# An attention mixer on one NeuronCore: recurrent projections from the first attention's end, the second attention's values last, no idle wide products, and 64-row products for two heads in turn

## Chip and metric

One core of a Trainium2 chip runs the whole program. The metric is the device time of one execution in microseconds (us), as the median over runs. TensorE multiplies (granted clock 1.2 or 2.4 GHz), VectorE and ScalarE do elementwise work, GpSimd some of it, and SyncE issues the loads of weights.

## What is computed

512 tokens of width 1024 in float32 pass two hybrid layers, a feed-forward layer, one mixer layer and another feed-forward layer. The change lies in the mixer layer. Its projections `p = u @ w_in` feed a pooling, two gated linear attentions (called `hgrn` and `gla`) and an RWKV-7 recurrence, each of four heads of 64:

```python
p_pool, p_hg, p_rw, p_gla = jnp.split(p, [G, 5 * G, 5 * G + RWKV_COLS], axis=-1)
# gated linear attention, for each chunk of 64
b = jnp.cumsum(gc, axis=-2)
scores = einsum(qc, kc, exp(b_t - b_s) for s <= t)
o = scores @ vc + (qc * exp(b)) @ S
# RWKV-7, for each token
S = S * w_t - (S kk_t)(kk_t * a_t)^T + v_t k_t^T ;  o_t = S r_t
```

For the recurrence the projections are mixed with those of the token before (`rwkv_mu`); the decay goes through tanh, a 64-wide product, a sigmoid and an exponential, `a` through a product and a sigmoid, the gate through a sigmoid and a 128-wide product, and the keys are normalised for each head.

## The kernel before

Everything is written by hand: each engine has its own instruction list, in its own order, and waits for the others at named events. Each engine runs its list in order. What one list has in front of an instruction therefore delays it, whether it depends on it or not.

A wide projection is one "unit" of weights (128 x 1024 float32). SyncE loads it to one of four `raw` buffers, ScalarE rounds it (`w_high`), VectorE takes the rest (`w_low`), both up to three units ahead (`use()`), and TensorE does 24 products with 512 moving columns, three for each of eight k tiles. `projected()` makes 128 features for all tokens; `token_major()` makes the values, four units into four PSUM banks that it holds until the last unit is done.

The eight banks go round in order (`take(key, freed_by)`): TensorE waits until the named event has freed the next one.

`linear_attention(name, fill)` works through nine levels, `ORDER` = 32, 16, 8, 4, 2, 1, 64, 128, 256 (the distance of the blocks that a level connects). For a level n VectorE makes the differences of the summed decay (`logs`), ScalarE their exponential (`factor`), VectorE the product with keys and queries (`factors`), TensorE the scores of pairs of blocks (`scores`), and VectorE (sizes up to 64, a predicated copy into `sb_near`) or ScalarE (128 and 256, into `sb_far`) takes them out. The near products, blocks on the diagonal, come first; the mixed products with the values `v2` come last. Between levels `fill(n)`, n = 0 to 9, puts other work in: one wide unit on TensorE as a rule, and what that unit asks of the other engines. Level n+1's factors are made, then `fill(n+1)` runs, then `scores(n)`. The factors have two buffers, `sb_E`.

Before, `fill_hgrn` has the first attention's values (4 units), the pooling's output products, the second attention's five feature projections, and at n = 8 and 9 two units of the second attention's values. `fill_gla` has the other two value units and the eight recurrent projections within n = 0 to 5. For n = 6 to 9 it runs `operand_steps()`: decay, gates, norms and exponentials of the recurrence, with no wide unit. In that part and behind it TensorE also does products that nobody reads (`keep_busy`, 128 x 512 float32): three ahead of the last level, one after it, five after the mixed products.

Then `inverse()`: for each head the gram products `AT` and `X` (64 contraction rows, 4 tiles of 128 x 128 columns), transposes of the operands (`turn_operands`), and VectorE's masks of them onto presets that ScalarE writes. Then five sizes 2 to 32, each with `Pm`, `X` and `XT` products for each head. `side_products()` puts the grams `A_ak`, `M_rk`, `M_rb` and the product `Gv` between them. Then `recurrence()`, eight chunks, with the output projection between.

A head of 64 rows sits on rows 0 to 63 or 64 to 127 of the array (`head_tile`): even and odd heads are on different halves. In the `scores` of sizes up to 64 two heads already go in turn, product by product. In the near, far and gram products one head's products all come before the next head's. A float32 product leaves two records in the trace.

Of the kernel before, what the change touches and what calls it, by code (L numbers as in the profile page):

```python
# [35 lines left out]
ORDER = (32, 16, 8, 4, 2, 1, 64, 128, 256)  # L36
HALF_E = math.exp(-0.5)
ROUND = 12582912.0
HEADS = range(4)
LAYERS = 2  # L40
# [101 lines left out]
def unit_order(t):  # L142
# [23 lines left out]
    values, projections = mixer_group(1), mixer_tiles(*range(2, 10))  # L166
    order += values[0:3] + [projections[0], values[3]] + projections[1:]
# [19 lines left out]
class Memory:  # L187
# [71 lines left out]
    def mixers(self, region, rotary_at, xg_at, phase_at, end):  # L259
# [8 lines left out]
        m.ga = r.room("ga", SEQ)  # L268
        m.y_tok = {name: r.room(f"y_{name}", TT, G) for name in ("hgrn", "rwkv", "gla")}
        first_at = r.at  # L270
        m.operands = {}
        for name in ("hgrn", "gla"):
# [3 lines left out]
            if name == "hgrn":  # L276
                second_at = r.at
        factors_at = r.at
# [11 lines left out]

        r = region(first_at, second_at)
        m.mixed = r.room("mixed", 8, SEQ)
        m.shifted = r.room("shifted", 2, SEQ)
        r = region(xg_at, phase_at)
        m.kkE, m.rE, m.bI, m.kI = (r.room(n, 2, SEQ) for n in ("kkE", "rE", "bI", "kI"))
        tok_at = r.at
        m.tokA, m.tokB = r.room("tokA", TT, 512), r.room("tokB", TT, 512)
        r = region(tok_at, phase_at)
        m.sigma, m.cum, m.a_gate, m.tmp = (r.room(n, 2, SEQ) for n in ("sigma", "cum", "a_gate", "tmp"))
# [4 lines left out]
        r = region(first_at, kept_at)  # L304
        m.M_rk, m.M_rb = (r.room(n, 4, TT * P) for n in ("M_rk", "M_rb"))
# [105 lines left out]
def tensor_engine(e, s, mem, units):  # L411
# [334 lines left out]
    def keep_busy(n):  # L746

        i = take(("unread", turn[0]), None)
        for _ in range(n):
            e.matmul(banks[i][:, :], mem.ones, mem.inv_rms, start=True, stop=True)  # L750

    def mixers():
# [1955 lines left out]
```

## Time and profile before

| | us |
|---|---|
| median of 3 runs | 1781.59 (1779.49 to 1781.84) |
| profiled execution, its own time | 1780.97 |
| its span | 1779.2 |
| TensorE busy in the span | 1716.0 (96%) |
| VectorE, ScalarE busy | 875.6, 675.5 |

The span runs from the first to the last instruction of the profiled execution; all times below are counted from its start. The changed part lies between about 1003 and 1313 us. TensorE's "busy" includes the products nobody reads.

### The profile page before, as it was taken

The numbers are of one execution on the slowest core, as the hardware profiler recorded it, in microseconds if no ns is written. First come the engines' busy times: TensorE is split into PE (matmuls) and PEld (weight loads), VectorE is DVE, ScalarE is ACT, GpSimd is POOL, SyncE is SP. The second block draws the span as 40 slices with busy tenths as digits, with TensorE's granted clock in tenths as the row PEclk, the third lists the DMA queues.
The fourth block names the chain that finished last, engine by engine and source line by source line (L and its number), as shares of the span: only waits on it lengthen the run. The fifth ranks groups of instructions, "written<-read, shape, count | busy, mean of one in ns | idle before, by whom it ended". The sixth has DMA issues, their size and how long they took to land.

```text
span 1779.2 us, 22284 instructions
## 1 busy us (share of the span) xinstructions
PE 1716.0 (96%) x8770; PEld 1396.2 (78%) x8770; DVE 875.6 (49%) x1169; ACT 675.5 (38%) x1017; POOL 129.3 (7%) x126
## 2 busy tenths in 40 slices
PE   7999999999999899999999899989998899999997
PEld 6777778878778788888888688868987688888886
DVE  5633445633445565444334676765345554444333
ACT  5145564225555333333223553463132433333221
POOL 0001002001000100000002200001320200000000
PEclk9999999999999999999999899987999999999998
DMA  5422213322212233233333222100011223223331
GB/s 187 129 71 72 83 48 97 120 92 84 71 61 73 70 107 95 95 100 96 96 96 134 71 63 68 60 19 1 1 30 36 83 90 100 95 98 96 91 98 57
DMA packets 40745, 143.92 MB, mean 81 GB/s; under 512 B 4816, under 2 KB 4832, under 8 KB 40384
## 3 DMA queue, kind: packets, MB, share of 16 engines
q1 hardware_dynamic: 37008, 130.87, 22.9%
q0 software_dynamic: 2192, 8.73, 1.6%
q10 hardware_dynamic: 1440, 2.88, 0.4%
q8 instruction: 70, 1.15, 0.3%
q14 instruction: 35, 0.29, 0.1%
HBM read 140.37 MB, written 2.10 MB: 80 GB/s over the span
## 4 chain that ended last, share of the span: by engine, by line
PE 84%; DVE 10%; ACT 4%; issue 1%; DMA 0%; POOL 0%; DVEq 0%; ACTq 0%; SPq 0%
PE bank L450 23%; PE bank L451 22%; PE bank L452 22%; PE bank L432 8%; PE bank L438 2%; DVE sb_w_low L1133 2%; PE bank L789 1%; DVE sb_rot L1133 1%; PE bank L668 1%; PE bank L647 1%; PE bank L604 1%; DVE sb_xg_low L1141 1%; ACT sb_w_high L1872 1%; DVE sb_x L1133 1%; PE bank L527 0%
## 5 line engine op out<-in xcount | busy, mean ns | idle before, releaser
L1133 DVE TENSOR_TENSOR sb_w_low<-sb_raw,sb_w_high 128x1024 fp32r<-128x1024 f32 (+1 forms) x253 | 310.0, 1225 | 390.0 <-ACT sb_w_high L1872 384.0
L450 PE MATMUL bank<-sb_xg_high,sb_w_high 128*128 128x512 f32 x1176 | 468.1, 398 | 23.5 <-DVE sb_xg_low L1141 15.6
L451 PE MATMUL bank<-sb_xg_low,sb_w_high 128*128 128x512 f32 x1176 | 460.8, 392 | 0.0
L452 PE MATMUL bank<-sb_xg_high,sb_w_low 128*128 128x512 f32 x1176 | 460.8, 392 | 0.0
L1872 ACT ACTIVATE sb_w_high<-sb_raw 128x1024 fp32r<-128x1024 f32 (+1 forms) x253 | 263.4, 1041 | 354.7 <-PE bank L452 324.2
L450 PEld LDWEIGHTS bank<-sb_xg_high,sb_w_high 128*128 128x128 f32 x1176 | 222.4, 189 | 89.2 <-issue 31.0
L452 PEld LDWEIGHTS bank<-sb_xg_high,sb_w_low 128*128 128x128 f32 x1176 | 222.4, 189 | 47.7
L451 PEld LDWEIGHTS bank<-sb_xg_low,sb_w_high 128*128 128x128 f32 x1176 | 222.6, 189 | 44.3
L452 PE MATMUL bank<-sb_h_high,sb_w_low 128*128 128x512 f32 x352 | 136.9, 389 | 0.0
L450 PE MATMUL bank<-sb_h_high,sb_w_high 128*128 128x512 f32 x352 | 136.9, 389 | 0.0
L451 PE MATMUL bank<-sb_h_low,sb_w_high 128*128 128x512 f32 x352 | 136.9, 389 | 0.0
L2440 POOL TENSOR_TENSOR sb_square_sum<-sb_square_sum,sb_square 128x512 f32<-128x512 f32 x34 | 45.3, 1333 | 958.3 <-ACT sb_square L1872 882.2
L450 PE MATMUL bank<-sb_w_high,sb_xg_high 128*128 128x512 f32 x256 | 103.9, 406 | 0.5 <-DVE sb_w_low L1133 0.4
L451 PE MATMUL bank<-sb_w_low,sb_xg_high 128*128 128x512 f32 x256 | 100.6, 393 | 0.0
L452 PE MATMUL bank<-sb_w_high,sb_xg_low 128*128 128x512 f32 x256 | 100.3, 392 | 0.0
L451 PEld LDWEIGHTS bank<-sb_h_low,sb_w_high 128*128 128x128 f32 x352 | 66.1, 188 | 13.8
L452 PEld LDWEIGHTS bank<-sb_h_high,sb_w_low 128*128 128x128 f32 x352 | 66.1, 188 | 13.8
L450 PEld LDWEIGHTS bank<-sb_h_high,sb_w_high 128*128 128x128 f32 x352 | 66.1, 188 | 13.5
L1872 ACT ACTIVATE sb_h_high<-sb_up 128x512 fp32r<-128x512 f32 x44 | 27.8, 633 | 118.4 <-DVE sb_up L1133 118.4
L1133 DVE TENSOR_TENSOR sb_up<-bank,sb_inv_rms 128x512 f32<-128x512 f32 x44 | 30.4, 692 | 81.2 <-PE bank L452 80.6
L1872 ACT ACTIVATE sb_gate<-sb_gate 128x512 f32<-128x512 f32 x44 | 27.8, 633 | 95.2 <-DVE sb_gate L1133 95.2
L450 PEld LDWEIGHTS bank<-sb_w_high,sb_xg_high 128*128 128x128 f32 x256 | 48.5, 189 | 19.2 <-issue 8.2
(336 smaller groups left out, 2110.1 us busy)
## 6 DMA issues: line engine op xcount, KB each, us to landing
sb_raw<-w_ffn_in SPq DMA_DIRECT2D x88, 512.0 KB, 3.3
sb_raw<-w_ffn_out SPq DMA_DIRECT2D x32, 512.0 KB, 3.5
sb_raw<-w_tok SPq DMA_DIRECT2D x24, 512.0 KB, 3.9
sb_raw<-w_mix_f SPq DMA_DIRECT2D x18, 512.0 KB, 3.3
sb_raw<-w_rot SPq DMA_DIRECT2D x16, 512.0 KB, 3.7
sb_raw<-w_qk SPq DMA_DIRECT2D x16, 512.0 KB, 3.3
sb_raw<-w_out SPq DMA_DIRECT2D x16, 512.0 KB, 3.3
sb_raw<-w_ffn_out SPq DMA_DIRECT2D x16, 384.0 KB, 3.1
```

What stands on the lines that cost most here:

```text
L432: made = e.matmul(out, lhsT, rhs, start=n == 0, stop=n == len(pairs) - 1)
L438: made = e.transpose(banks[i][:, blk(n)], in_, mem.ident)
L450: e.matmul(out, w[0], v[0], start=first, stop=False)
L451: e.matmul(out, w[0], v[1], start=False, stop=False)
L452: return e.matmul(out, w[1], v[0], start=False, stop=last)
L604: made = e.matmul(out[k], m.feat["rk"][r, f, blk(j)], m.feat["rq"][r, f, j * P:], start=part == 0, stop=part == 1)
L647: e.matmul(out[k], m.qT[r, j, blk(q)], m.kT[r, j, 0:keys], start=True, stop=True).then_inc(*p.up("scores", n, 2 * j + k, q))
L668: made = e.matmul(out[64 * k:64 * k + 64, blk(q)], m.tok["av"][:, key, h * ATT_DIM:(h + 1) * ATT_DIM], m.probT[:, 2 * (q % 2) + k, blk(key ...
L789: made = e.matmul(banks[i][:, at:at + 64].rearrange("p (n c) -> p n c", c=size), et, halves(et, size, True), start=True, stop=True)
L1133: e.tensor_tensor(out, a, b, op).then_inc(*v.up(*signal))
L1872: e.activation(out, in_, func, bias=bias, scale=scale, accum_out=accum).then_inc(*a.up(*signal))
L2440: e.tensor_tensor(out, a, b, op).then_inc(*g.up(*signal))
```

## The change

- The recurrent projections come in the order 6, 7, 2, 3, 0, 1, 4, 5 (features: decay and `a`, gate, keys, receptance, values). Two take the places n = 8 and 9 of `fill_hgrn`, six n = 0 to 5 of `fill_gla`. The second attention's four value units take n = 6 to 9 of `fill_gla`.
- `operand_steps` is taken apart. Its steps stand at single n: decay and gate products at the end of the first attention, sigmoids with n = 0 of the second, decay sums n = 1, key squares and exponentials n = 2, key norm n = 3, key spread n = 5, keys n = 6 and 7, receptance n = 8 and 9. Some operands get other places in memory. The second attention's output copy on ScalarE waits for `rE`.
- `keep_busy` is gone.
- Near, far and gram products go through two heads in turn, tile by tile.
- In the first attention ScalarE does `fill(0)` ahead of `factor(0)`.
- The second attention's output gate (Silu) moves from `fill_gla(4)` to behind its root in the inverse.

The diff, cut:

```diff
+RWKV_ORDER = (6, 7, 2, 3, 0, 1, 4, 5)
-    values, projections = mixer_group(1), mixer_tiles(*range(2, 10))
-    order += values[0:3] + [projections[0], values[3]] + projections[1:]
+    order += mixer_tiles(*(2 + f for f in RWKV_ORDER)) + mixer_group(1)
@@ TensorE, attention
             fill(0)
-            for h in HEADS:
-                r, g = head_tile(h)
-                i = take(("near", name, h), ("near", name, h))
-                p.wait_ge(*of("decay summed", name, 1))
+            p.wait_ge(*of("decay summed", name, 1))
+            for two in HEAD_PAIRS:
+                out = [take(("near", name, h), ("near", name, h)) for h in two]
                 for t in range(TT):
-                    group(banks[i][:, blk(t)], [(k2[r, g, blk(t)], q2[r, g, blk(t)])], "near product", name, h)
+                    for h, i in zip(two, out):
+                        r, g = head_tile(h)
+                        made = e.matmul(banks[i][:, blk(t)], k2[r, g, blk(t)], q2[r, g, blk(t)], start=True, stop=True)
+                        if t == TT - 1:
+                            made.then_inc(*p.up("near product", name, h))
...
-                    for h in HEADS:
-                        r, g = head_tile(h)
-                        i = take(("pairs", name, n, h), ("far", name, n, h))
-                        if size == 128:
-                            for k, key in enumerate((0, 2)):
-                                group(banks[i][:, blk(k)], [(x2[r, g, blk(key)], x2[r, g, blk(key + 1)])],
-                                      "pairs", name, n, h)
-                        else:
-                            for key in range(2):
-                                group(banks[i][:, key * 256:(key + 1) * 256],
-                                      [(x2[r, g, blk(key)], x2[r, g, 256:512])], "pairs", name, n, h)
+                    for two in HEAD_PAIRS:
+                        out = [take(("pairs", name, n, h), ("far", name, n, h)) for h in two]
+                        for k in range(2):
+                            for h, i in zip(two, out):
+                                r, g = head_tile(h)
+                                if size == 128:
+                                    made = e.matmul(banks[i][:, blk(k)], x2[r, g, blk(2 * k)], x2[r, g, blk(2 * k + 1)],
+                                                    start=True, stop=True)
+                                else:
+                                    made = e.matmul(banks[i][:, k * 256:(k + 1) * 256], x2[r, g, blk(k)],
+                                                    x2[r, g, 256:512], start=True, stop=True)
+                                if k:
+                                    made.then_inc(*p.up("pairs", name, n, h))
-                if name == "gla" and n == len(ORDER) - 1:
-                    keep_busy(3)
                 scores(n)
-            if name == "gla":
-                keep_busy(1)
             fill(len(ORDER))
             last = len(ORDER) - 1
             for half in range(2):
                 i = take(("mixed", name, half), ("mixed landed", name, half))
                 p.wait_ge(*of("near done", name))
-                p.wait_ge(*of("far", name, last, 3))
-                p.wait_ge(*of(landed("v", 3), name, 3))
+                p.wait_ge(*of("far", name, last - 1 + half, 3))
@@ TensorE, fills
+                next(values_h if n < 3 else others if n < 8 else projections)
+            if n == 9:
+                decay_and_gate_in()
 
         linear_attention("hgrn", fill_hgrn)
...
+            next(projections if n < 6 else values_g)
+            if n == 1:
+                gate_out()
+            if n == 3:
+                key_norm()
+            if n == 6:
+                key_turned()
+            if n == 9:
+                p.mark("xg read", MIX_NORM)
         linear_attention("gla", fill_gla)
-        keep_busy(5)
@@ TensorE, inverse
+        def gram(what, two, left, right):
+
+            out = [take((what, h), {"AT": ("XT made", 2, h), "X": ("X made", 2, h)}.get(what, (what, h))) for h in two]
             p.wait_ge(*of(*before_products))
             for t in range(TT):
-                group(banks[i][:, blk(t)], [(left[r, f, blk(t)], right[r, f, blk(t)])], what + " product", h)
+                for h, i in zip(two, out):
+                    r, f = head_tile(h)
+                    made = e.matmul(banks[i][:, blk(t)], left[r, f, blk(t)], right[r, f, blk(t)], start=True, stop=True)
+                    if t == TT - 1:
+                        made.then_inc(*p.up(what + " product", h))
...
+        for two in HEAD_PAIRS:
+            gram("AT", two, m.bI, m.kkE)
+            if not two[0]:
+                bonus_sums(0)
+                bonus_sums(1)
+            gram("X", two, m.kkE, m.bI)
+            if not two[0]:
+                bonus_sums(2)
+                bonus_sums(3)
+            for t in two:
+                turn_operands(t)
...
+            for two in HEAD_PAIRS:
+                gram("A_ak", two, m.kI, m.kkE)
+                yield
+                for h in two:
+                    v_cols = slice(G + h * 64, G + (h + 1) * 64)
+                    p.wait_ge(*of("A_ak", h))
+                    p.wait_ge(*of("tokB", TT - 1))
+                    per_tile(("Gv product", h), ("Gv", h), tile_of(m.A_ak[:, h % 2, :]),
+                             lambda t: m_tokB(t, v_cols), cols64)
+                    yield
...
+                gram("M_rk", two, m.kI, m.rE)
+                yield
+                gram("M_rb", two, m.bI, m.rE)
@@ VectorE, second attention
+            if n == 0:
+                finish_hgrn()
+            if n == 3:
+                key_floor()
+            next(projections if n < 6 else values_g)
+            if n == 1:
+                decay_sums()
+            if n == 6:
+                keys_scaled()
+            if n == 7:
+                keys()
+            if n == 8:
+                receptance()
+            if n == 9:
+                receptance_faded()
@@ ScalarE, attention
-            factor(0)
-            fill(0)
+            if name == "hgrn":
+                fill(0)
+                factor(0)
+            else:
+                factor(0)
+                fill(0)
...
+            if name == "gla":
+                a.wait_ge(*of("rE"))
@@ ScalarE, fills
+            if n == 9:
+                decay_in()
...
+        def gates():
+            a.wait_ge(*of("y made", "hgrn"))
             for f in range(2):
                 for what, out, bias in (("sigma", m.sigma, "rwkv_w0"), ("a gate", m.a_gate, "rwkv_a0")):
                     a.wait_ge(*of(what + " in", f))
                     act(out[:, f, :], bank(what, f)[:, :], what, f, func=ACT.Sigmoid, bias=mem.col(bias, f))
-            act(m.mixed[:, 7, :], m.mixed[:, 7, :], "rwkv sigmoid", func=ACT.Sigmoid)
-            a.wait_ge(*of("key norm"))
-            a.wait_ge(*of("key inverse"))
-            act(heads(flat(m.kI)), small[:, 176:192].unsqueeze(2).to_broadcast([P, 16, 64]), "key spread")
-            yield
+            a.wait_ge(*of("rwkv mixed", 7))
+            act(m.gates_in[:, 1, :], m.gates_in[:, 1, :], "rwkv sigmoid", func=ACT.Sigmoid)
...
+            if n == 0:
+                finish_hgrn()
+                gates()
+            if n == 2:
+                key_squares()
+                decay_exps()
+            if n == 5:
+                key_spread()
+            next(projections if n < 6 else values_g)
+            if n == 1:
+                gate_out()
...
+        def gla_out():
+            finish_gla()
+            bend_gate("gla")
+
+        inverse(m, gla_out)
```

Not shown: VectorE's masks for two heads in turn, ScalarE's copies of `Gv` in the same order, and the two new rooms `gates_in` and `shifted`, which lie where the second attention's values come later.

## Rows read from the trace of the kernel before

**Rows 1.** The page, part 1: busy time, share of the span, instructions.

```profile
PE 1716.0 (96%) x8770; PEld 1396.2 (78%) x8770; DVE 875.6 (49%) x1169; ACT 675.5 (38%) x1017; POOL 129.3 (7%) x126
```

**Rows 2.** Stretches: length, busy time of each engine (instructions), granted clock, DMA.

```profile
1005.20:1017.20 12.00, 5.03 (x34) 4.83 (x32) 8.29 (x9) 6.27 (x7) 0.00 (x0) 0.59 0.28 88
...
1097.90:1164.20 66.30, 66.30 (x402) 54.66 (x401) 48.79 (x56) 31.40 (x34) 0.00 (x0) 1.00 0.20 62
1164.20:1209.00 44.80, 37.90 (x268) 27.84 (x267) 31.86 (x35) 26.82 (x39) 3.44 (x1) 0.89 0.03 10
1209.00:1232.70 23.70, 23.70 (x113) 21.85 (x114) 11.03 (x14) 5.41 (x10) 2.54 (x2) 0.57 0.00 0
1232.70:1303.20 70.50, 69.11 (x579) 66.45 (x578) 26.58 (x51) 15.85 (x29) 24.27 (x21) 1.00 0.00 1
```

**Rows 3.** TensorE in time: start, length, instruction, count, idle before and its releaser.

```profile
1012.18 5.13 PE L432 MATMUL bank<-sb_kq_hgrn 64*128 64x128 f32 x32 [6.97 <-ACT sb_y_pool L1872]
...
1156.60 2.00 PE L789 MATMUL bank<-sb_E 64*128 64x64 f32 x32
...
1164.20 3.79 PE L789 MATMUL bank<-sb_E 64*128 64x64 f32 x64
...
1195.32 1.30 PE L432 MATMUL bank<-sb_v_gla,sb_near 128*128 128x64 f32 x10 [0.40 <-ACT sb_far L1872]
...
1204.27 4.51 PE L750 MATMUL bank<-sb_inv_rms,sb_ones 128*128 128x512 f32 x10
1208.98 1.16 PE L432 MATMUL bank<-sb_kkE,sb_bI 64*128 64x128 f32 x8 [0.20 <-DVE sb_rE L1133]
...
1236.03 1.11 PE L432 MATMUL bank<-sb_Pm,sb_XT 128*128 128x64 f32 x8 [1.39 <-ACT sb_Pm L1872]
```

**Rows 4.** ScalarE in time, start of the first attention.

```profile
1002.60 1.28 ACT L1872 ACT_TABLE_LOAD   x1
1007.84 1.06 ACT L1872 ACTIVATE sb_E<-sb_E 128x1024 f32<-128x1024 f32 x1 [3.95 <-DVE sb_E L1133]
...
1011.35 3.38 ACT L1872 ACTIVATE sb_y_pool<-bank,sb_small,sb_cols 64x512 f32<-64x512 f32 x4
```

**Rows 5.** VectorE in time, the same stretch.

```profile
1003.87 2.48 DVE L1153 TENSOR_TENSOR_SCAN sb_c_hgrn<-sb_mixer,sb_c_hgrn 128x512 f32<-128x512 f32 x2
```

**Rows 6.** Groups of TensorE, 1098 to 1304: busy, mean ns | idle before.

```profile
L432 PE MATMUL bank<-sb_kkE,sb_kI 64*128 64x128 f32 x32 | 4.6, 285 | 0.0
...
L432 PE MATMUL bank<-sb_mixed,sb_lora 64*128 64x512 f32 x8 | 3.6, 1055 | 2.9 <-ACT sb_mixed L1872 2.9
```

**Rows 7.** Groups of VectorE, 1098 to 1209.

```profile
L1531 DVE COPY_PREDICATED sb_near<-sb_mixer,bank 128x512 f32<-128x512 int32 x14 | 12.5, 892 | 0.5
```

**Rows 8.** VectorE in time, one level of the second attention.

```profile
1142.14 1.22 DVE L1133 TENSOR_TENSOR sb_E<-sb_E,sb_kq_gla 128x1024 f32<-128x1024 f32 x1
1143.47 1.23 DVE L1133 TENSOR_TENSOR sb_w_low<-sb_raw,sb_w_high 128x1024 fp32r<-128x1024 f32 x1
1144.80 0.69 DVE L1133 TENSOR_TENSOR sb_shifted<-bank,sb_inv_rms 128x512 f32<-128x512 f32 x1
1146.28 0.75 DVE L1141 SCALAR_TENSOR_TENSOR sb_mixed<-sb_shifted,sb_cols,sb_mixed 128x511 f32<-128x511 f32 x1 [0.79 <-ACT sb_mixed L1872]
1147.14 1.42 DVE L1133 TENSOR_TENSOR sb_E<-sb_c_gla 128x512 f32<-128x512 f32 x2
1148.59 1.48 DVE L1531 COPY_PREDICATED sb_near<-sb_mixer,bank 128x512 f32<-128x512 int32 x2
1150.17 1.23 DVE L1133 TENSOR_TENSOR sb_E<-sb_E,sb_kq_gla 128x1024 f32<-128x1024 f32 x1
```

**Rows 9.** VectorE in time, first head of the inverse.

```profile
1210.46 0.69 DVE L1133 TENSOR_TENSOR sb_AT<-bank,sb_mixer 128x512 f32<-128x512 f32 x1 [1.53 <-ACT sb_XT L1872]
```

**Rows 10.** ScalarE in time, the second attention's root.

```profile
1233.77 1.28 ACT L1872 ACT_TABLE_LOAD   x1
1235.07 0.22 ACT L1872 ACTIVATE sb_small<-sb_small 128x16 f32<-128x16 f32 x1
```

More of the change, by code:

```diff
@@ L39 @@
 HEADS = range(4)
+HEAD_PAIRS = ((0, 1), (2, 3))
 LAYERS = 2
@@ L851, in gla_steps, with rwkv_steps, decay_and_gate_in, gate_out @@
                 yield
-        values_h, others, values_g = token_major("v", "hgrn", 1, n), gla_steps(), token_major("v", "gla", 1, n)
+        def rwkv_steps():
+            for f in RWKV_ORDER:
+                projected("rwkv", f, "rwkv landed", f)
+                yield
+        projections = rwkv_steps()
+        values_h, others = token_major("v", "hgrn", 1, n), gla_steps()
+        def decay_and_gate_in():
+            for f in range(2):
+                for what, r in (("sigma", slice(0, 64)), ("a gate", slice(64, 128))):
+                    i = take((what, f), (what, f))
+                    p.wait_ge(*of("rwkv tanh"))
+                    group(banks[i][:, :], [(m.lora[r, 0, blk(f)], m.gates_in[r, 0, :])], what + " in", f)
+        def gate_out():
+            for half in range(2):
+                i = take(("gate out", half), ("g tok", half))
+                p.wait_ge(*of("rwkv sigmoid"))
+                for j in range(2):
+                    group(banks[i][:, j * G:(j + 1) * G], [(m.gates_in[:, 1, blk(2 * half + j)], m.lora[:, 1, :])],
+                          "gate out", half)
+        def key_norm():
+            i = take(("key norm",), ("key floored",))
+            p.wait_ge(*of("key squares"))
+            for t in range(TT):
+                for f in range(2):
+                    at = 4 * t + 2 * f
+                    group(banks[i][:, at:at + 2], [(m.rv[:, f, blk(t)], mem.table("same_head")[:, 0:P:64])],
+                          "key norm")
+        def key_turned():
+            for f in range(2):
+                i = take(("key turned", f), ("key scaled", f))
+                p.wait_ge(*of("key spread"))
+                transposes(i, [flat(mem.square)[:, blk(2 * t + f)] for t in range(TT)], "key turned", f)
         def fill_hgrn(n):
@@ L1729, in side_products @@
         def side_products():
[L1730 to L1733 removed]
+            for two in HEAD_PAIRS:
+                for h in two:
+                    if h >= 2:
+                        v.wait_ge(*of("Gv product", h - 2))
+                    masked("A_ak", m.A_ak[:, h % 2, :], h, mem.table("before"))
                 yield
[L1735 removed]
                 yield
[L1737 removed]
+                yield
+                for h in two:
+                    masked("M_rk", m.M_rk[:, h, :], h, mem.table("upto"))
+                yield
+                for h in two:
+                    masked("M_rb", m.M_rb[:, h, :], h, mem.table("upto"))
                 yield
@@ L2225, in gla_steps, with rwkv_steps, decay_in @@
             yield
-        values_h, others, values_g = value_steps("hgrn"), gla_steps(), value_steps("gla")
+        def rwkv_steps():
+            for k, f in enumerate(RWKV_ORDER):
+                use()
+                a.wait_ge(*of("rwkv landed", f))
+                a.wait_ge(*of("kept"))
+                if f in (4, 5):
+                    a.wait_ge(*of("key norm"))
+                act(m.own[f], m.shifted[:, k % 2, :], "rwkv own", f, scale=small[:, 100 + f:101 + f])
+                yield
+        def decay_in():
+            a.wait_ge(*of("rwkv mixed", 6))
+            act(m.gates_in[0:64, 0, :], m.gates_in[0:64, 0, :], "rwkv tanh", func=ACT.Tanh)
+        projections = rwkv_steps()
+        values_h, others = value_steps("hgrn"), gla_steps()
         def fill_hgrn(n):
+            if n == 9:
+                decay_in()
             if n == 0:
```

254 lines of the change are left out of this document (77 added, 177 removed).

## Prediction

> **What bounds the kernel now.** I read the page first, then the stretches of the mixer stage, then TensorE, ScalarE and VectorE in time, then the groups for sizes of single operations. Over the whole span TensorE is busy 96% [rows 1], so nothing but less TensorE work, less idle TensorE or a higher clock can pay. The change touches only the part from 1003 to 1313 us. There the stretches differ [rows 2]: from 1097.9 to 1164.2 TensorE is full at clock 1.00; before that, from 1005.2 to 1017.2, it is busy 5.0 of 12 us at clock 0.59; from 1164.2 to 1209.0 it is busy 37.9 of 44.8 us at 0.89, and some of that "busy" is filler; from 1209.0 to 1232.7 it is always busy, but at 0.57, so near 1.2 GHz most of the time. From 1232.7 to 1303.2 it is full again at 1.00. The largest single wait is 6.97 us for ScalarE's `y_pool`, before the near products [rows 3].
>
> **Start of the first attention.** Why is `y_pool` late? Not for its own sake: ScalarE loads a table at 1002.60, is done at 1003.88, then idles 3.95 us for VectorE's log, does the exponential, two weight halves, and only then the four `y_pool` copies, 1011.35 to 1014.73 [rows 4]. VectorE cannot be sooner: scans to 1006.35 [rows 5], logs until the exponential starts at 1007.84 [rows 4]. The change puts `fill(0)` ahead of `factor(0)`. The two weight halves (they fill the 2.4 us between the exponential and `y_pool`) then run from 1002.6 to 1004.9 and the four copies (3.4 us) to 1008.3. A near product needs a bank freed by such a copy and the scans: the first pair starts at 1006.7, the second at 1008.3, and wide products resume at 1009.4 (each pair of near products 1.1 us, see the pairs below), not at 1017.3 (near products of 5.13 us from 1012.18, at half clock [rows 3]). That is 7.9 us. The wide products after 1017.3 also ran at the low clock for some 3.7 us, which costs 1.8 us more. If the clock stays up the gain is 9.7 us; if it falls as before for a while in the 6 us without wide products, some 3 us are given back. Between 6.5 and 9.7 I take **-8.5 us**. The exponential comes later instead (table, 1.28 us, and 1.06 us after 1008.3: 1010.7), VectorE's product at 1011.9; its reader on TensorE stands behind a wide unit that ends at 1014.9, so that is covered by 3 us.
>
> **Rest of the first attention.** One level is one wide unit and 32 records of pairs: 7.60 us from the pairs of one level at 1156.60 to those of the next at 1164.20, 2.0 of them the pairs [rows 3]. The same number of units is left in. Moved in are the products for the decay and the gate `a`, 3.6 us of record at half clock and two row halves in turn already [rows 6], so 1.8 us at full clock; two heads in turn in the far products give back some 0.5 us (9 steps of one row half become 8, in two levels). Tanh (table 1.28, 0.63) lies under the 5.4 us of unit 7. With changes of operand shape I take **+1.6 us**.
>
> **Second attention: does VectorE keep up?** Here I put the most work, since VectorE was busy 48.8 of 66.3 us while TensorE was full [rows 2], and the change hangs the decay sums, the keys and the receptance between its levels. Let 0 be the end of the first attention's last products (1097.9). ScalarE's copy, square, sum, root and three multiplications, 1.22 us each as the 128x1024 product of [rows 8], put "y made" at 6.5. Five sigmoids on ScalarE (a `y_pool` copy, half the rows, took 0.85 [rows 4]; I take 0.75) end at 10.3; only then comes `use()`, so the next weight half is at 11.4 and its low part on VectorE at 12.6 (VectorE idles 5 us for it). Near products meanwhile wait for banks that the sigmoids free: TensorE idles some 2.4 us.
> Level 1 on VectorE, with the durations of the step in [rows 8] and a tenth of a us between two: landing, product, four near masks (0.7 as the landing), mix, logs, a wait for the exponential, product: 9.9, so factors(1) at 22.5. Level 2: low part 1.3, landing 0.8, decay sums 3.8 (scans 2.5 [rows 5], subtraction 1.2), mix 0.8, logs 1.45, copies 1.5, product 1.3: factors(2) at 33.5. Level 3: ScalarE does key squares and three exponentials (4.7 us) before the next weight half, so VectorE waits 4.3 us, and the rest is 7.9: 45.7. Levels 4 to 6 carry the same work as the step measured at 1142.14 to 1150.17, 8.03 us [rows 8]; with 1.1 us more for the predicated copy at size 2 (the 14 copies average 0.89 us [rows 7] and not the 0.74 us of this step) and 0.7 less for one log: 70.2. Level 7: low part, keys scaled 1.65, logs, copies 2.7, product: 78.6. Level 8: low part 1.3, `keys()` 3.8 (three operations of 1.23), logs 1.45, copies 1.5, product 1.3: **factors(8) at 88.0**.
> TensorE's own work up to there is nine units (49), near products 2.4, gate, norm and turned keys 5.0, seven levels of pairs 15, one far level 1.2: 72.6 us. So VectorE, not TensorE, sets the end, by 15 us spread over the stage, and the last 7 to 9 us of it in one piece before the last far products: TensorE has just read factors(7), the last unit is placed behind `scores(8)`, and nothing stands between. The clock falls there. After 88.0: far products 3.6 (half clock; 2.0 at full), the last unit 7.4 (5.45 at full), ScalarE's copy of the values 1.0, mixed products 9.0 as at 1195.32 to 1204.27 [rows 3]: the first 64-row gram product at 109.4. Before it was 1208.98 - 1097.9 = 111.1. Receptance and `rE` (eight operations of at most 1.23 us on VectorE, under 10 us) lie under those 21 us. The filler matmuls (the last five: 4.51 us from 1204.27 [rows 3]) cost nothing before, since they stood in waits (the first gram waits for `rE` even after them), so their removal gives nothing. **-1.6 us**: the idle 15 us swallow what the move of the values hides.
>
> **Head of the inverse.** Presets still follow the last mixed product (6.2 us, VectorE's wait for `XT` ends at 1210.46 [rows 9]); then VectorE needs 2.3 us a head, a mask of 0.69 [rows 9] and two predicated copies of 0.74 as in [rows 8], 9.2 for four. Paired grams at 1.1 us for two heads lie under that. Then square and sum 2.5, root, and new on ScalarE a Silu table and the gate (1.28 and 1.07) ahead of the first `Pm` copy: updates(0) 21.1 us after the grams begin, and some 2 us of low clock behind so much waiting: 23.1. Before: 1236.03 - 1208.98 = 27.05. **-4.0 us**. Bounds: 21.1 with the clock up, 27 if the drop lasts.
> Here a row and a rule differ. The load at 1233.77 takes 1.28 us and its user starts at 1235.07, 0.02 us after it [rows 10]. The Trainium skill, "ScalarE: Activation LUTs", section "What ACT_TABLE_LOAD costs", adds about 1.38 us of drain to each switch, 2.66 in all; by it the two new switches in a chain (sigmoid ahead of the gates, Silu ahead of `Pm`) would cost 2.8 us more: 1765.3, within the forecast's own range and no case of its own. The sum goes by the row.
>
> **Inverse loop.** Twelve gram products (`A_ak`, `M_rk`, `M_rb`, four heads each) fill TensorE there: 32 records of one kind are 4.6 us of record time [rows 6], and one head's eight take 1.08 us start to start. For two heads in turn the pairs are the row to read: 32 records, 16 on each row half, in 2.0 us, 0.06 a record, where one head's eight take 1.16 with their end, 0.14 a record [rows 3]. So a pair of heads costs what one did: 6 x 1.08 = **-6.4 us** after 0.1 for waits. Size 32 ran without fillers before and hardly waited (69.1 busy of 70.5 [rows 2]), so shorter fillers need not open gaps. The recurrence is untouched.
>
> **Sum.** -8.5 + 1.6 - 1.6 - 4.0 - 6.4 = -18.9. The profiled execution took 1780.97 us (span 1779.2), 0.6 below the median 1781.59. I predict 1762.5 us.
>
> **Rivals.** (a) TensorE bounds the second attention: VectorE's idle 5.0 and 4.3 us shrink and the levels overlap better. For it: today VectorE has 17.5 us to spare in the 66.3 us where TensorE is full [rows 2]. Against: the chain above has hardly a free choice. It gives up to 15 us more; 1748 to 1756. (b) The reorder at the first attention pays nothing, since the low clock or the scans take over: 1771. (c) Low clock from the big wait lasts through the mixed products and grams, as the 20 us before 1232.7 did: +10, 1773. (d) Two heads in turn don't overlap at 128 columns as they do at 64: no gain in the loop, 1769. (e) The other side: each level of the second attention pays a round trip between VectorE and ScalarE that the mix and the extra operations lengthen. At 8.0 us a level it is as forecast; from 10 us a level in all ten levels (+20) the kernel is no faster, at 10.5 it ends at 1787. The rows of one step [rows 8] speak against: that round trip (0.79 us of wait for `mixed`) is in the 8.03.
> Less than 0.2% (3.6 us) is about what a measurement here cannot tell from no change.
>
> **Numbers.** Forecast 0.45 (own range 1757 to 1768), (a) 0.20, (b) 0.12, (c) 0.10, (d) 0.05, (e) 0.05, nothing measurable 0.03. 1750 to 1773 leaves out (e), no change and the low end of (a), under 0.2. Faster 0.92, same 0.03, slower 0.05.
>
> **What would show it.** `y_pool` copies ahead of the first exponential, wide products back before 1010; one long TensorE wait for VectorE's `sb_E` before the last far products with the clock down after it; the 16 records of two heads' grams in about 1.1 us; `Pm` waiting behind a Silu table. I am wrong if TensorE is full through the second attention, or if the clock, not VectorE, sets its length.

## The result, and the profile after

The changed kernel takes 1769.77 us (median of 4 runs, 1765.24 to 1770.69) against 1780.54 us (4 runs, 1779.12 to 1781.84) before: a ratio of 0.9935, 95% interval 0.9915 to 0.9954, so 10.8 us faster. The forecast of 1762.5 had the sign right and promised 18 us; the measured time lies 1.8 us above the range that it gave itself (1757 to 1768). The profiled execution was the fastest of the four, 1765.24 us with a span of 1763.2 us (from its first to its last instruction); its three neighbours took 1769 to 1771.

The busy shares of the changed kernel, from the page, hardly move: TensorE loses 26.5 us (1.5%) of its busy time and keeps its share of the span [rows 1].

```profile
PE 1689.5 (96%) x8752; PEld 1376.3 (78%) x8752; DVE 875.3 (50%) x1169; ACT 673.6 (38%) x1016; POOL 129.0 (7%) x126
```

The stretches of the changed kernel, cut at marks on TensorE: the pool's product ahead of the first attention, the first products of `sb_E` (L796), the last mixed product of the first attention, the first one of the second, the first gram product, the first of `Pm`, the first of the recurrence (`Gv`), its last transposes. Columns as in [rows 2]: length, busy time and count on TensorE, its weight loads, VectorE, ScalarE, GpSimd, then granted clock, DMA share, GB/s.

```profile
1002.60:1017.80 15.20, 12.91 (x67) 9.26 (x66) 12.71 (x16) 8.21 (x10) 0.00 (x0) 0.78 0.22 70
1017.80:1093.10 75.30, 74.75 (x540) 60.98 (x540) 55.54 (x60) 36.57 (x44) 0.00 (x0) 1.00 0.20 64
1093.10:1194.20 101.10, 87.81 (x563) 71.39 (x563) 77.83 (x86) 44.25 (x56) 2.93 (x1) 0.90 0.15 45
1194.20:1203.30 9.10, 9.07 (x82) 9.03 (x82) 0.00 (x0) 2.57 (x4) 0.00 (x0) 1.00 0.01 2
1203.30:1226.40 23.10, 14.81 (x130) 13.67 (x129) 13.86 (x17) 15.03 (x23) 5.73 (x4) 0.85 0.00 1
1226.40:1289.20 62.80, 62.80 (x560) 61.51 (x561) 23.56 (x48) 12.88 (x23) 21.62 (x19) 0.95 0.00 1
1289.20:1366.20 77.00, 69.61 (x413) 56.11 (x413) 44.45 (x88) 23.16 (x44) 8.18 (x5) 1.00 0.13 42
```

The same marks were read in the trace of before (some of them in [rows 2, 3]), in a second run of the changed kernel (`e1_after_again`, called "again" below), and in the best of the experiments (`e10_before_pairs_order`, below). The table gives the stages in us. It goes by the hundredths of the marks, so a value can differ by 0.1 from the stretches above.

| stage | before | forecast | after | again | e10 |
|---|---|---|---|---|---|
| unchanged work ahead of it | 1003.3 | 0 | 1002.6 | 1003.3 | 1001.1 |
| start of the first attention | 21.3 | -8.5 | 15.1 | 13.6 | 15.2 |
| rest of it | 73.2 | +1.6 | 75.4 | 76.2 | 73.2 |
| second attention to the mixed products | 97.5 | | 101.1 | 100.2 | 97.4 |
| mixed products, fillers, to the grams | 13.7 | -1.6 for both | 9.0 | 9.0 | 13.7 |
| head of the inverse | 27.0 | -4.0 | 23.1 | 23.2 | 15.7 |
| loop of the inverse | 67.1 | -6.4 | 62.8 | 62.3 | 61.3 |
| recurrence | 80.0 | 0 | 77.0 | 80.0 | 77.0 |
| from there to the end | 396.0 | 0 | 397.0 | 397.5 | 396.6 |
| span | 1779.2 | -18.9 | 1763.2 | 1765.3 | 1751.3 |

The recurrence takes 80.0 or 77.0 us in these and the other traces below (78.6 in `e3_grams_in_row`); the code there is the same. The 3.0 us are two stretches of low clock that an execution has or has not (`e3_grams_in_row` has one). They make the profiled execution of the changed kernel look better than its median, so "again" is the fairer column for the stages. Even so, one trace against another overstates the change: before and again differ by 13.9 us in span, and by 11.4 in the medians of that session.

**The start.** TensorE and ScalarE in the changed kernel, from the pool's product (start, duration; in brackets the idle time and what ended it):

```profile
1002.63 1.93 PE L442 MATMUL bank<-sb_window,sb_pool_w 64*64 64x512 f32 x8
1006.28 1.16 PE L783 MATMUL bank<-sb_kq_hgrn 64*128 64x128 f32 x16 [1.72 <-ACT sb_y_pool L1898]
1008.01 2.08 PE L783 MATMUL bank<-sb_kq_hgrn 64*128 64x128 f32 x16 [0.57 <-ACT sb_y_pool L1898]
1010.02 0.79 PE L460 MATMUL bank<-sb_w_high,sb_xg_high 128*128 128x512 f32 x1
```
```profile
1002.15 2.23 ACT L1898 ACTIVATE sb_w_high<-sb_raw 128x1024 fp32r<-128x1024 f32 x2
1004.49 3.37 ACT L1898 ACTIVATE sb_y_pool<-bank,sb_small,sb_cols 64x512 f32<-64x512 f32 x4
1007.94 1.28 ACT L1898 ACT_TABLE_LOAD   x1
1009.24 1.06 ACT L1898 ACTIVATE sb_E<-sb_E 128x1024 f32<-128x1024 f32 x1
```

The wait for `y_pool` fell from 6.97 us [rows 3] to 1.72 and 0.57, and wide products are back at 1010.0.

**The second attention.** What TensorE waited for from 1093.1 to 1194.2 (line and bank; tile awaited; total, times, longest; its four largest), and three moments of VectorE:

```profile
PE bank L460 <- DVE sb_near L1543: 3.6, 1, 3.6
PE bank L807 <- DVE sb_near L1543: 2.1, 1, 2.1
PE bank L783 <- ACT sb_sigma L1898: 1.9, 2, 1.5
PE bank L460 <- DVE sb_w_low L1145: 1.8, 1, 1.8
```
```profile
1181.34 1.22 DVE L1145 TENSOR_TENSOR sb_E<-sb_E,sb_kq_gla 128x1024 f32<-128x1024 f32 x1
...
1191.40 1.23 DVE L1145 TENSOR_TENSOR sb_rE<-sb_rE,sb_eB 128x1024 f32<-128x1024 f32 x1
1209.36 0.69 DVE L1145 TENSOR_TENSOR sb_AT<-bank,sb_mixer 128x512 f32<-128x512 f32 x1 [16.74 <-ACT sb_XT L1898]
```

TensorE is idle for 13.3 of the 101.1 us. The eighth factors are done at 1182.56, 89.4 us after the end of the first attention's products. Behind them VectorE makes the receptance, up to `rE` at 1192.6. Then it has 16.7 us with nothing to do, after a stage in which it was the one that others waited for.

**The head of the inverse.** TensorE and ScalarE:

```profile
1203.27 1.16 PE L936 MATMUL bank<-sb_kkE,sb_bI 64*128 64x128 f32 x16
...
1213.21 2.08 PE L936 MATMUL bank<-sb_kkE,sb_bI 64*128 64x128 f32 x16 [1.69 <-DVE sb_XT L1740]
...
1226.40 1.97 PE L442 MATMUL bank<-sb_Pm,sb_XT 128*128 128x64 f32 x8 [4.59 <-ACT sb_Pm L1898]
```
```profile
1223.31 1.28 ACT L1898 ACT_TABLE_LOAD   x1
1224.60 1.06 ACT L1898 ACTIVATE sb_v_gla<-sb_v_gla 128x1024 f32<-128x1024 f32 x1
1225.75 1.28 ACT L1898 ACTIVATE sb_Pm<-bank 128x512 f32<-128x512 f32 x2
```

Sixteen records of two heads take 1.16 us, what eight of one head took [rows 3]. At the low clock the same sixteen take 2.08. `Pm` stands behind the Silu table and the gate, and its first reader on TensorE has waited 4.59 us.

### The profile page after: what moved, and what is told of

It reads as the page before. It is cut to its first block, busy times and chain, and to the rows that moved or that the text cites. A ratio compares the mean times of both kernels' runs of the same rounds, so it can differ in the third digit from the quotient of the medians.

```text
span 1763.2 us, 22257 instructions
## 1 busy us (share of the span) xinstructions
PE 1689.5 (96%) x8752; PEld 1376.3 (78%) x8752; DVE 875.3 (50%) x1169; ACT 673.6 (38%) x1016; POOL 129.0 (7%) x126
## 4 chain that ended last, share of the span: by engine, by line
PE 79%; DVE 14%; ACT 5%; issue 1%; DMA 0%; DVEq 0%; ACTq 0%; SPq 0%
PE bank L460 22%; PE bank L462 21%; PE bank L461 21%; PE bank L442 6%; DVE sb_w_low L1145 3%; DVE sb_E L1145 2%; PE bank L448 1%; ACT sb_w_high L1898 1%; PE bank L678 1%; PE bank L657 1%; PE bank L614 1%; DVE sb_near L1543 1%; DVE sb_xg_low L1153 1%; DVE sb_rot L1145 1%; DVE sb_x L1145 1%
## 5 line engine op out<-in xcount | busy, mean ns | idle before, releaser
L460 PEld LDWEIGHTS bank<-sb_h_high,sb_w_high 128*128 128x128 f32 x352 | 66.1, 188 | 13.7
L461 PEld LDWEIGHTS bank<-sb_h_low,sb_w_high 128*128 128x128 f32 x352 | 66.1, 188 | 13.7
L462 PEld LDWEIGHTS bank<-sb_h_high,sb_w_low 128*128 128x128 f32 x352 | 66.1, 188 | 13.7
```

Source lines behind the costliest of these rows:

```text
L460: e.matmul(out, w[0], v[0], start=first, stop=False)
L461: e.matmul(out, w[0], v[1], start=False, stop=False)
L462: return e.matmul(out, w[1], v[0], start=False, stop=last)
```

## The experiments

Three questions: is each part worth what the sum says, does VectorE set the length of the second attention, and what does the clock do at the grams? Each ratio below is to the kernel before, run on the same chip in the same session.

**The changed kernel again.** No edit.

> The changed kernel once more, with nothing edited, so that the edits beside it have a neighbour of the same session. If the 1765 to 1771 us of its runs come from how often the granted clock falls behind the waits, the runs should spread over some 5 us again, with the longer ones at a lower mean granted clock (0.976 beside 0.983). The rival, that the first run was merely a lucky one of a kernel that takes 1770, would show four of five runs or more at 1769 to 1771.

1768.18 us (5 runs, 1767.54 to 1768.78), ratio 0.9935 [0.9923, 0.9948]. This is the value that the others are set against. The runs spread over 1.2 us and not over 5, and none of them took 1769 or more: neither of the two expectations came true.

**Order at the first attention undone.** ScalarE's queue in the changed kernel:

```diff
-            if name == "hgrn":
-                fill(0)
-                factor(0)
-            else:
-                factor(0)
-                fill(0)
+            factor(0)
+            fill(0)
```

> The changed kernel with ScalarE's old order at the start of the first attention (exponential, then weight halves and y_pool copies). In the profile of the changed kernel this place gave 6.2 us (scores of level 0 at 1017.77 instead of 1024.61, both counted with 0.65 us earlier arrival). Theory: 6 to 7 us slower than the changed kernel, TensorE waits about 7 us for y_pool again and the low clock lasts 13.7 us instead of 6.8. Rival: the clock and VectorE's chain at the next levels take the gain back, under 2 us.

1776.11 us (11 runs), 0.9978 [0.9970, 0.9987]: 7.9 us slower than again. The start of the first attention takes 20.2 us instead of 13.6, so 6.6 us of it are there. In the same trace the clock is low from 1228.0 to 1241.6 at the start of the inverse's loop, twice as long as in again, and the loop takes 65.4 us instead of 62.3, though the edit does not touch it. The term of 8.5 stands in the main, and rival (b), that the order pays nothing, falls.

**Gram products one head after the other.**

```diff
-            for t in range(TT):
-                for h, i in zip(two, out):
+            for h, i in zip(two, out):
+                for t in range(TT):
```

> The changed kernel with the gram products of a pair one head after the other (near and far products still in turn). Theory: a pair costs 0.9 us more (eight further records on the same row half at 0.112 us), six pairs in the inverse loop where TensorE has no idle time: 5.4 us, and up to 1 us at the four pairs ahead of it, where VectorE sets the pace: 5 to 7 us slower than the changed kernel. Rival: the row halves share something else and the loop was helped by its order alone: under 2 us.

1780.5 us (11 runs), 1.0007 [0.9997, 1.0016]: 12.3 us slower than again, about twice the forecast term, and no faster than before. The loop took 76.6 us instead of 62.3. Its stretches (same columns) say where. From 1224.0, in the wait ahead of the loop, which begins at 1225.7, the clock is at 1.2 GHz for 30.7 us; the rest is at 2.4.

```profile
1224.00:1254.70 30.70, 28.96 (x136) 28.52 (x137) 6.74 (x12) 5.35 (x9) 5.06 (x4) 0.50 0.00 1
1254.70:1303.00 48.30, 48.30 (x432) 47.25 (x432) 18.69 (x38) 9.12 (x16) 17.10 (x16) 1.00 0.00 1
```

In the changed kernel the low stretch there ended at 1232.9. In this one it lasts until 1254.7, and TensorE is busy for every microsecond of its last 28. In it stand gram records such as these sixteen, one head's eight after the other's:

```profile
1236.28 3.09 PE L936 MATMUL bank<-sb_kkE,sb_kI 64*128 64x128 f32 x16
```

The two kernels differ in the order of these products alone. So the pairs save twice: the record time, and time at the low clock. The forecast had 6.4 us for the first; the loops differ by 14.3 us, which leaves, as an estimate, some 8 for the second.

**Keys later.** In VectorE's queue `keys()` moves from step 7 to 8 of the second attention, `receptance()` from 8 to 9:

```diff
-            if n == 7:
-                keys()
             if n == 8:
-                receptance()
+                keys()
             if n == 9:
+                receptance()
                 receptance_faded()
```

> The changed kernel with VectorE's keys() moved from n = 7 to n = 8 and receptance() from n = 8 to n = 9, both behind the last factors of the second attention; VectorE is idle 16.7 us there. Theory (VectorE's chain sets the second attention's length): the last factors come 3.7 us earlier, the last far products with them, and the kernel is 3.7 us faster, up to 6 us if the low clock behind the wait goes too. Rival (TensorE or the banks set it): 0, the wait moves to another event.

1763.05 us (4 runs), 0.9909 [0.9894, 0.9924]: 5.1 us faster than again. The second attention takes 95.8 us instead of 100.2: 3.7 us of `keys()` left the chain ahead of the eighth factors, and the stage is 4.4 us shorter.

```profile
1091.10:1186.90 95.80, 84.79 (x564) 69.35 (x563) 74.31 (x83) 44.32 (x56) 2.93 (x1) 0.93 0.15 47
```

So VectorE set the end of this stage. Two other stages differ by clock alone. The loop takes 65.3 us, 3.0 more than again's: the clock is low for 13.7 us from 1217.1. And the start of the first attention, which the edit does not touch, stayed at the full clock and took 12.0 us:

```profile
1003.10:1015.10 12.00, 9.86 (x65) 6.90 (x64) 10.70 (x13) 6.97 (x8) 0.00 (x0) 1.00 0.26 88
```

**The kernel before without its fillers.** `keep_busy(3)`, `keep_busy(1)` and `keep_busy(5)` are left out (products that nobody reads).

> The kernel before without its nine products that nobody reads, and nothing else. Prediction's theory (they stand in waits): within 1 us of the kernel before. Rival (they kept the clock up for the mixed products and the first grams, or cost time of their own): if they held the clock, the granted clock falls already before 1200 us and the kernel is 3 to 7 us slower; if they cost time, 1 to 3 us faster.

1784.38 us (8 runs), 1.0033 [1.0020, 1.0046]: 5.8 us slower than before. The clock falls at 1191.4 and stays low for 47.8 us, through the far products, the mixed products and the grams:

```profile
1191.40:1239.20 47.80, 47.02 (x203) 43.83 (x204) 21.75 (x26) 15.14 (x23) 2.54 (x2) 0.50 0.00 1
```

So the prediction's "their removal gives nothing" does not hold for the kernel before: the mixed products took 17.2 us without the five fillers behind them, and 13.7 with them. In the changed kernel the last wide unit stands ahead of the mixed products, and they ran at clock 1.00; that the unit is what kept the clock up there was not tested by itself.

**A filler at the wait for `Pm`.** In the changed kernel, at size 2, after the second product:

```diff
             product(1)
+            if size == 2:
+                i = take(("unread", turn[0]), None)
+                for _ in range(5):
+                    e.matmul(banks[i][:, :], mem.ones, mem.inv_rms, start=True, stop=True)
```

> The changed kernel with five unread 128x512 float32 products of TensorE put into the wait for the first Pm copy (4.6 us idle, low clock for 6.8 us from 1226.3). Theory that the low clock there is worth time: the updates behind it run at 1.00 and the kernel is 2 to 3.5 us faster. Rival: the fillers themselves run at the low clock and last longer than the wait (five at 1.7 us are 8.5): 0 to 4 us slower.

1762.31 us (4 runs), 0.9908 [0.9895, 0.9920]: 4.8 us less than again (by the ratios). The wait for `Pm` is filled, and the loop starts at the full clock and takes 59.7 us instead of 62.3. These 2.6 us are what the trace shows for the filler; the rest of the 4.8 was not found in a stage of its own:

```profile
1221.13 4.46 PE L1019 MATMUL bank<-sb_inv_rms,sb_ones 128*128 128x512 f32 x10
1225.99 1.11 PE L442 MATMUL bank<-sb_Pm,sb_XT 128*128 128x64 f32 x8 [0.40 <-ACT sb_Pm L1902]
```

**The head's work on ScalarE earlier.** In the changed kernel the preset of `X` goes ahead of the output copies, and the Silu gate between the copies of `tokA` and `tokB`:

```diff
             if name == "gla":
+                preset("X", m.X, "factors read")
                 a.wait_ge(*of("rE"))
...
-        preset("X", m.X, "factors read")
         preset("XT", m.XT, "mixed")
...
         for i in range(TT):
+            if i == 2:
+                bend()
```

Not shown: `gla_out`, which ran the gate behind the root, is gone.

> The changed kernel with two moves on ScalarE ahead of the inverse: the X preset before the output copies of the second attention (ScalarE is idle there), and the Silu gate between the copies of the turned operands instead of behind the root. Theory (the head of the inverse is a chain of ScalarE and VectorE): 2.6 us from the preset, 2.3 us from the gate, 5 us faster than the changed kernel. Rival (TensorE or the banks bound the head): under 1 us.

1761.74 us (4 runs), 0.9899 [0.9885, 0.9914]: 6.4 us less than again. The head takes 17.4 us instead of 23.2. The presets of `XT` start at 1202.37 and not at 1206.65, and behind the root comes `Pm` at once:

```profile
1209.68 1.28 ACT L1898 ACT_TABLE_LOAD   x1
1210.97 1.06 ACT L1898 ACTIVATE sb_v_gla<-sb_v_gla 128x1024 f32<-128x1024 f32 x1
...
1218.04 0.22 ACT L1898 ACTIVATE sb_small<-sb_small 128x16 f32<-128x16 f32 x1 [1.68 <-DVE sb_small L1161]
1218.35 1.28 ACT L1898 ACTIVATE sb_Pm<-bank 128x512 f32<-128x512 f32 x2
```

The loop behind it pays part of this back: 64.6 us instead of 62.3, at a mean clock of 0.92.

```profile
1219.00:1283.60 64.60, 64.60 (x561) 63.21 (x561) 25.68 (x49) 12.88 (x23) 22.00 (x20) 0.92 0.00 1
```

**Both, and the decay exponentials behind the weights.** The two edits above in one kernel, and `decay_exps()` moved from ahead of to behind the projection step at n == 2 on ScalarE.

> keys_late and head_early together, and decay_exps() on ScalarE behind the projection's step of n = 2 instead of ahead of it (VectorE waited 4.2 us for a weight half there; the three exponentials are 3.2 us). Theory: 3.7 + 5 + up to 3 us = 9 to 12 us faster than the changed kernel. Rival (the gains overlap, since each wait ends at the next engine's): no more than the better of the two alone.

1752.05 us (median of 6), 0.9878 [0.9841, 0.9915]; two of the six runs took 1764.79 and 1773.74, which is why the interval is wide. It is 10.1 us faster than again by the ratios and 16.1 by the medians, so the expected 9 to 12 cannot be confirmed closely. Second attention 94.5, head 17.1, loop 62.7 us.

**That kernel with a filler of two products at `Pm`.** As above, with `range(2)`.

> e8 (keys late, head early, exponentials late) with two unread products in the shortened wait for the first Pm copy. The low clock of 6.8 us from 1212.6 in e8 costs up to 3.4 us there. Theory (the filler keeps the clock up): 2 to 3 us faster than e8, 1749 to 1750. Rival (what is left of the wait is too short for a filler, and its own 1 to 3 us stand on the path): 1 to 3 us slower.

1755.7 us (4 runs), 0.9869 [0.9848, 0.9889]: not to be told from the one without. The profiled loop took 59.7 us instead of 62.7, so the clock effect is there. But in the same trace the recurrence took 80.0 us and not 77.0, the four runs lie 6.4 us apart, and the gain does not show in them.

**The kernel before with the gram pairs alone.** The new `gram`, the loops over `HEAD_PAIRS` (with them the places of bonus sums and transposes between the grams) and the order of side products on TensorE, VectorE and ScalarE; projections, values, fillers, near and far products as before.

> The kernel before with one part of the change alone: its gram products in the inverse for two heads in turn (order of projections, fillers and near and far products as before). Theory: 5.4 us in the loop as computed for single heads in row, and at the head of the inverse VectorE instead of TensorE at the low clock sets the pace, 27.0 us become 17 to 19: together 13 to 16 us faster than the kernel before, about 1764, so more than the whole change gave. Rival (the head was freed by the move of the projections, not by the pairs): the first grams stay at the low clock and only the 5 to 7 us of the loop are gained.

1760.86 us (4 runs), 0.9892 [0.9877, 0.9907]: 20.1 us faster than before, nearly twice the whole change, where 13 to 16 were expected. The head fell from 27.0 to 15.7 us and stayed at the full clock, the loop from 67.1 to 61.3:

```profile
1206.80:1222.50 15.70, 11.92 (x129) 10.98 (x129) 11.82 (x16) 8.35 (x15) 5.81 (x4) 1.00 0.01 2
1222.50:1283.80 61.30, 61.30 (x560) 60.01 (x561) 25.62 (x49) 12.88 (x23) 21.89 (x20) 0.97 0.00 1
```

**Pairs and the order at the first attention alone.** The kernel above with `fill(0)` ahead of `factor(0)` for the first attention on ScalarE.

> As e9, and ScalarE's new order at the start of the first attention too. If the parts add up: 7 us below e9, near 1757, which would be 11 us faster than the changed kernel without any projection moved. Rival (the low clock takes back what the start gives): within 3 us of e9.

1753.3 us (4 runs), 0.9852 [0.9837, 0.9867]: the fastest kernel of the study but for the equal one of three edits above, 27.7 us faster than before. It leaves out most of what gives the change its name: projections, values and fillers stay where they were. Four of its stretches, from the second attention to the loop:

```profile
1089.50:1186.90 97.40, 93.31 (x579) 74.85 (x578) 70.64 (x79) 50.08 (x63) 3.44 (x1) 0.93 0.15 47
1186.90:1200.60 13.70, 13.47 (x91) 10.76 (x91) 9.98 (x11) 8.07 (x11) 0.00 (x0) 1.00 0.00 1
1200.60:1216.30 15.70, 11.93 (x128) 10.98 (x128) 11.79 (x16) 8.38 (x15) 5.78 (x4) 1.00 0.01 2
1216.30:1277.70 61.40, 61.38 (x561) 60.09 (x561) 25.68 (x49) 12.88 (x23) 22.01 (x20) 0.97 0.00 1
```

## Why the prediction was right, and where it was not

The terms first, against again: start -7.7 (forecast -8.5), rest of the first attention +3.0 (+1.6), second attention to the grams -2.0 (-1.6), head -3.9 (-4.0), loop -4.8 (-6.4), recurrence 0, the end +1.5 (0). They add up to -13.9, 5.0 short of -18.9; the other 3 us to the measured 10.8 lie between the two profiled executions and the medians. The measured 1769.8 is beside the prices of rival (d), 1769, and (b), 1771, but by chance: neither took place (`e3_grams_in_row`, `e2_order_back`).

**Start of the first attention, -8.5: right.** Measured in this stage -6.2 in the profile, -7.7 again; by medians of whole kernels -7.9 by undoing it, -7.6 by adding it alone. The `y_pool` copies ended at 1007.86 (forecast 1008.3), wide products were back at 1010.0 (1009.4), in a trace in which the stage began 0.65 us earlier. The clock fell at 1007.7 all the same; how long it stays down (6.8 us in one trace, 3.4 in another) is the spread between the first two. In the trace of `e4_keys_late` it did not fall there, and the stage took 12.0 us, -9.3: the prediction's bounds of 6.5 and 9.7, low clock and full clock, were both nearly met.

**Rest of the first attention, +1.6: too small.** +2.2 and +3.0. The sum's 1.8 us of products moved in are most of it; the second trace has 3.4 us at the low clock from 1036.3 on, and is 0.8 us longer. What else the stage took is not known.

**Second attention, -1.6: right in size and mechanism, wrong in shape.** From the end of the first attention to the grams it took 110.1 us (109.2 again) against 111.2; the eighth factors came at 89.4 against 88.0; TensorE was idle for 13.3 us against 15 in the sum. (The sum's last step is off: 88.0, 3.6, 7.4, 1.0 and 9.0 make 109.0 and not 109.4, so the term should have been -2.1.) `e4_keys_late` shows that VectorE's chain sets the end, so rival (a), TensorE as the bound, falls. Rival (e), ten microseconds or more a level, falls by the length of the stage. But the one long wait of 7 to 9 us ahead of the last far products did not come. The longest wait, 3.6 us, stands in the middle of the stage at 1153.7 and is a wide unit's wait for a bank that VectorE's `near` copy frees; the waits before the last two levels are 2.1 and 0.8 us. The last far products start at 1183.1, 0.5 us after their factors. The clock fell three times (1130.5, 1151.0, 1181.7) and not once.

**Head of the inverse, -4.0: right.** Forecast 23.1, measured 23.1 and 23.2: `Pm` behind the Silu table, `XT` behind eight presets. As the sum allowed for, part of it is at the low clock: 6.8 us from 1212.5. The Trainium skill, "ScalarE: Activation LUTs", section "What ACT_TABLE_LOAD costs", adds about 1.38 us of drain to a switch. The trace does not agree: here the load at 1223.31 takes 1.28 us and its user starts 0.01 us after it, so the row was the right price.

**Loop, -6.4: the records right, the clock missed.** Measured -4.3 and -4.8. With the clock up it is 59.7 us (`e6_filler_at_pm`), -7.4. About 2.6 to 3.1 us of that are lost because the wait for `Pm` (4.6 us) is followed by 6.8 us at the low clock, from 1226.1 on, where the sum had put "some 2 us" and ended it with the head.

**The step that failed** is the one that priced the pairs by record time alone. The text knew that the 23.7 us at the single-head grams ran at clock 0.57 [rows 2] and took this as rival (c), a nuisance that might last. In the trace of before TensorE is busy all the time and at 1.2 GHz from 1211.9 to 1232.4:

```profile
1211.90:1232.40 20.50, 20.50 (x91) 18.91 (x91) 9.32 (x13) 3.81 (x7) 2.05 (x2) 0.50 0.00 0
```

The prediction never asked what the pairs do to this. They are worth 12.3 us in the changed kernel (`e3_grams_in_row`) and 20.1 in the one before (`e9_before_gram_pairs`). In the latter's trace 5.8 us are the loop and 11.3 the head, at clock 1.00 and with shorter grams; 3.0 are the recurrence's clock, which no part of the change is known to set. (Its span is 21.7 us shorter; another 2.6 lie ahead of 1003, in unchanged code, and two stages took back 1.0.)

**So what do the moves bring?** The sum gave them no column of its own. Compare again with `e10_before_pairs_order`, which differ in the moves, the fillers, and the near and far products in turn, whose share was not measured by itself. From the first level to the grams it is 76.2 + 100.2 + 9.0 = 185.4 us against 73.2 + 97.4 + 13.7 = 184.3: the projections and values fill what fillers filled, and gain nothing. Behind this the head is 7.5 us longer and the loop 1.0. In the kernel of pairs and order alone the eight presets (1196.72 to 1201.98) run under mixed products and fillers and are done before the second gram product; the moves took that cover off, and put presets and Silu gate into the chain to `Pm`. By the ratios, across two sessions, the changed kernel is 14.7 us slower than `e10_before_pairs_order`; the spans differ by 14.0. Of these 9.6 are the head, the loop and the 1.1 us above; 3.0 are the recurrence's clock, whose cause I did not find, 2.2 lie ahead of 1003 in unchanged code, 0.9 at the end, and the start was 1.6 shorter. So the moves cost some 10 us that can be placed. `e3_grams_in_row` says the same from the other side: with the order at the first attention (worth 7.6 alone) but without the gram pairs the changed kernel is no faster than before. `e7_head_early` gives 6.4 us back, `e4_keys_late` 5.1, and with both and the exponentials the kernel comes level with the one without moves: 1752.05 against 1753.3 us, ratios 0.9878 and 0.9852 with overlapping intervals. Whether like edits would also help the kernel without moves was not tried.

**Open.** Why the recurrence has its two low stretches in some kernels' executions and not in others; and the 1.0 to 1.5 us behind 1366, in unchanged code. That the order of the gram products sets how long the clock stays down is shown by `e3_grams_in_row`, where nothing else differs; what it is in single-head grams that does so was not isolated.

## What to carry to other kernels

Price a change of operation order by its clock too: read the granted clock of the stretch, and ask what the new order does to it; here that was about half of the gain or more. When a change bundles several parts, sum each part separately and ask of each whether the others would do better without it: moved work that only replaced fillers gained nothing here, and it uncovered what lay under them. When an engine's chain sets a stage and the engine is idle right after, push all that the stage's end does not need behind it.

## What the runs showed of the hardware

- 64-row products of two heads in turn run beside each other at 128 columns: 16 records in 1.16 us against 8 in 1.16. The Trainium skill, "TensorE: Matmul & The Clock Gate", section "Part 3: Packing small matmuls — row/col tiling", describes such concurrency for tiles on different rows; the trace agrees.
- With grams of one head after the other TensorE was busy all the time and yet at 1.2 GHz: for 20.5 us before, and for 28 us in `e3_grams_in_row`. With pairs the head of `e9_before_gram_pairs` had clock 1.00, with TensorE busy for 11.9 of 15.7 us. In the changed kernel, whose head has longer waits (busy 14.8 of 23.1 us), the mean was 0.85.
- Products that nobody reads, put into waits, held the clock and were worth more than they cost: 5.8 us before, 4.8 at `Pm`, where the stretch behind them ran at 1.00. At a wait that was already short, 2.6 us, they gave nothing that runs can tell (0.9869 against 0.9878).
- The same code ran at different clocks in different executions: the start of the first attention took 15.1, 13.6 and 12.0 us in three traces, with 6.8, 3.4 and 0 us at 1.2 GHz.
